# A hybrid decoder layer on one Trainium2 core: a second copy of x with columns as rows, and 1 / rms sent through DRAM

## The reference, cut to what matters

```python
h = rmsnorm(x, ln_gain)                      # x: 2048 tokens x 1024 channels
z = einsum('bsd,de->bse', h, w_in)           # 1024 -> 4608 columns
q, k, v, g_attn, x_lru, g_lru = split(z)
y_attn = rmsnorm(swa_sink_attention(rope(q), rope(k), v, sinks) * silu(g_attn), attn_out_gain)
u      = causal_depthwise_conv(x_lru, conv_w, conv_b)
y_lru  = rmsnorm(rg_lru(u, gates) * silu(g_lru), lru_out_gain)
x      = x + concat([y_attn, y_lru]) @ w_out
out    = rmsnorm(x, final_gain)
# rmsnorm(x, g) = x * rsqrt(mean(x * x) + EPS) * g, per token
```

## Time and profile before

| | |
|---|---|
| median of 3 runs | 1374.45 us |
| profiled execution | 1375.38 us |
| its span, first to last instruction | 1373.7 us |
| PE busy | 1353.7 us (99%) |
| DVE busy | 970.2 us (71%) |
| ACT busy | 845.6 us (62%) |
| granted TensorE clock | 0.998 of full speed |

### The profile page before, as it was taken

The page is one execution under the profiler, slowest core; times in us unless marked ns, Lnnn a source line. Parts: engine busy times, 40 slices in busy tenths (PEclk is TensorE's granted clock), DMA queues, the critical chain, the costliest instruction groups (busy, mean ns, idle before and its releaser), DMA issues.

```text
span 1373.7 us, 22283 instructions
## 1 busy us (share of the span) xinstructions
PE 1353.7 (99%) x6756; PEld 1107.4 (81%) x6756; DVE 970.2 (71%) x1668; ACT 845.6 (62%) x1729; POOL 217.2 (16%) x247
## 2 busy tenths in 40 slices
PE   8999999999999999999999999999989999999998
PEld 7777877888888888888888878888867888888886
DVE  5998999968686877868687767878686544434442
ACT  7888797867777685867777585766764221222120
POOL 2020212112130312113031212213020000000000
PEclk9999999999999999999999999999999999999999
DMA  8766768655554555454555655354535423324120
GB/s 323 260 226 246 274 225 288 230 188 173 183 178 177 203 184 200 158 187 172 184 186 184 224 202 211 135 206 164 193 114 193 138 86 97 98 86 121 62 92 31
DMA packets 98289, 243.22 MB, mean 177 GB/s; under 512 B 8112, under 2 KB 43056, under 8 KB 98224
## 3 DMA queue, kind: packets, MB, share of 16 engines
q1 hardware_dynamic: 91200, 217.79, 46.9%
q0 software_dynamic: 7024, 24.65, 4.5%
HBM read 179.49 MB, written 62.91 MB: 176 GB/s over the span
## 4 chain that ended last, share of the span: by engine, by line
PE 85%; DVE 3%; ACT 2%; issue 1%; DMA 1%; DVEq 0%; ACTq 0%; POOL 0%; POOLq 0%
PE ring L1548 50%; PE acc_b L223 12%; PE ring L223 11%; PE ps_tv L1611 4%; PE ps_s L1587 3%; PE ps_tv L1598 2%; PE ring L1625 2%; PE ps_tv L1587 1%; PE ring L1635 1%; DMA y_scratch<-ya 1%; PE ring L1560 0%; DMA w_raw<-w_out_d 0%; DVE o_sb L1318 0%; PE acc_b L1998 0%; DVE cu L1340 0%
## 5 line engine op out<-in xcount | busy, mean ns | idle before, releaser
L1548 PE MATMUL ring<-split,w_hi 128*128 128x512 f32 x2288 | 717.1, 395 | 1.1 <-DVE w_lo L1082 0.4
L1548 PEld LDWEIGHTS ring<-split,w_hi 128*128 128x128 f32 x2288 | 421.3, 188 | 97.5 <-issue 8.9
L1548 PE MATMUL ring<-split,w_lo 128*128 128x512 f32 x1144 | 446.6, 390 | 0.0
L1548 PEld LDWEIGHTS ring<-split,w_lo 128*128 128x128 f32 x1144 | 214.7, 188 | 45.9
L663 POOL TENSOR_SCALAR_AFFINE_SELECT p_hi_c<-p_hi 128x512 fp32r<-128x512 f32 x64 | 41.5, 648 | 518.1 <-ACT p_hi L891 518.1
L883 ACT ACTIVATE p_sb<-s_sb,smax 128x129 f32<-128x129 f32 x256 | 99.6, 392 | 0.6
L1840 ACT ACTIVATE w_hi<-res 128x1024 fp32r<-128x1024 f32 x15 | 15.9, 1060 | 132.3 <-DVE res L1913 132.3
L223 PE MATMUL acc_b<-wo_rest,y_own 128*128 128x512 f32 x384 | 90.8, 393 | 5.4 <-DVE rms L1898 4.3
L223 PE MATMUL ring<-split,y_own 128*128 128x512 f32 x384 | 91.5, 392 | 0.0
L1340 DVE SCALAR_TENSOR_TENSOR cu<-xl,prm,cu 128x512 f32<-128x512 f32 x96 | 72.2, 752 | 26.6 <-ACT cu L910 20.0
L223 PEld LDWEIGHTS acc_b<-wo_rest,y_own 128*128 128x128 f32 x384 | 72.2, 189 | 21.3 <-DVE rms L1898 4.4
(11 more groups left out here) (249 smaller groups left out, 2420.5 us busy)
## 6 DMA issues: line engine op xcount, KB each, us to landing
w_hi<-w_split_scratch SPq DMA_DIRECT2D x108, 512.0 KB, 3.3
w_lo<-w_split_scratch SPq DMA_DIRECT2D x108, 512.0 KB, 4.3
w_raw<-w_tiles_d SPq DMA_DIRECT2D x36, 512.0 KB, 4.3
w_split_scratch<-w_hi SPq DMA_DIRECT2D x36, 512.0 KB, 5.0
w_split_scratch<-w_lo SPq DMA_DIRECT2D x36, 512.0 KB, 5.7
y_scratch<-hs POOLq DMA_DIRECT2D x32, 256.0 KB, 6.2
y_scratch<-ya POOLq DMA_DIRECT2D x16, 512.0 KB, 6.0
rows<-y_scratch SPq DMA_DIRECT2D x8, 1024.0 KB, 7.8
```

Source lines behind the costliest of these rows:

```text
L1548: last = mm(bank(r), w[:, i % WSLOTS, k, :], h[:, par, k, :], start=(k == 0 and j == 0), stop=(k == KC - 1 and j == 2))
```

## The change

The input is given a second time, as `x_turned`, laid out on the host with the 128 channels of a piece on the partitions and the tokens along the rows. SP now loads a block of both forms (two transfers of 512 KB instead of one). The first form only serves the sum of squares. The second one, `xt`, takes the half of `rows` in which the gain lay, and is normalised where it is: 1 / rms, one number for each of 128 tokens on the partitions, must become a row on every partition. It is stored to DRAM and read back to all partitions (`rs_row`), and DVE multiplies in eight instructions of 128x128, one for each piece, with the gain as a scalar per partition. ACT and DVE then split `xt` in SBUF. The turns on TensorE in the bodies, their two places in the ring and the load of the gain go away.

```diff
-    xb = both.rows[:, 0, :];  gain_row = both.rows[:, 1, :]
+    xb = both.rows[:, 0, :];  xt = both.rows[:, 1, :].rearrange("p (k t) -> p k t", k=KC)
             def load_x(g, q):
                 sp.dma_start(xb, x[0, bass.ds((g + (q + 1) * KV) * P, P), :]).then_inc(*x_in.one())
+                sp.dma_start(xt, x_turned[bass.ds(g + (q + 1) * KV, 1), :, :, :].rearrange("o p k t -> p (o k) t")
+                             ).then_inc(*x_in.one())
                 load(GA0)
+                if q < NQUART - 1:
+                    sp.wait_ge(*x_rs.at(n, 1))
+                    sp.wait_ge(*x_norm.at(n, 0))
+                    sp.dma_start(rs_dram.rearrange("o p -> p o"), xs[:, 3:4]).then_inc(*rs_kept.one())
                 load(GA1)
+                if q < NQUART - 1:
+                    sp.wait_ge(*rs_kept.at(n, 1))
+                    sp.dma_start(rs_row[:, :], rs_dram.broadcast_to([P, P])).then_inc(*rs_in.one())
                 load(GL1)
...
                 if x_follows(q, nxt_par != par):
-                    sp.wait_ge(*ring_ready.at(n, R_XT1 + 1))
+                    sp.wait_ge(*h_low.at(n, 2))
                     load_x(following, q + (nxt_par != par))
...
             def square_x(n):
-                act.wait_ge(*x_in.at(n, 1))
+                act.wait_ge(*x_in.at(n, 2))
...
+            def invert_x(n):
+                dve.wait_ge(*x_root.at(n, 0))
+                dve.wait_ge(*rs_kept.at(n, 0))
+                nc.vector.reciprocal(xs[:, 3:4], xs[:, 2:3]).then_inc(*x_rs.one())
             def norm_x(n):
-                dve.wait_ge(*x_root.at(n, 0))
-                nc.vector.reciprocal(xs[:, 3:4], xs[:, 2:3]).then_inc(*x_rs.one())
-                dve.wait_ge(*x_rs.at(n, 1))
-                stt(out=xb, in0=xb, scalar=xs[:, 3:4], in1=gain_row, op0=ALU.mult,
-                    op1=ALU.mult).then_inc(*x_norm.one())
+                dve.wait_ge(*x_in.at(n, 0))
+                dve.wait_ge(*rs_in.at(n, 1))
+                for c in range(KC):
+                    last = stt(out=xt[:, c, :], in0=xt[:, c, :], scalar=prm[:, C_GAIN, c:c + 1], in1=rs_row[:, :],
+                               op0=ALU.mult, op1=ALU.mult)
+                last.then_inc(*x_norm.one())
...
                 sink_in()
+                if q < NQUART - 1:
+                    invert_x(n)
                 conv(0)
...
                 lru_tail(0)
-                lru_scan(0)
                 if split_next:
                     split_w(n, KVG)
+                lru_scan(0)
...
                 turn_p(0)
-                if q < NQUART - 1:
-                    turn_x()
                 score(3)
...
                 if nxt_par != par:
-                    pe.wait_ge(*ring_dve.at(n, FREED_BY_DVE.index(R_XT1) + 1))
+                    pe.wait_ge(*h_low.at(n, 2))
```

More of the change, by code:

```diff
@@ L112, in two @@
         return self.sem, 2 * self.unit
-    def three(self):
-        self.count += 3
-        return self.sem, 3 * self.unit
     def checked(self, bodies, beyond=0):
@@ L280, in phase_a @@
     xb = both.rows[:, 0, :]
-    gain_row = both.rows[:, 1, :]
+    xt = both.rows[:, 1, :].rearrange("p (k t) -> p k t", k=KC)
     h_hi = both.split[:, :, 0, :].rearrange("p q (k t) -> p q k t", k=KC)
@@ L391, in phase_a @@
         ring_dve = signal("ring_dve", len(FREED_BY_DVE))
-        x_in = signal("x_in", 1, 16, ahead=1)
+        x_in = signal("x_in", 2, 16, ahead=2)
+        rs_kept = signal("rs_kept", 1, 16)
+        rs_in = signal("rs_in", 1, 16)
         x_sq = signal("x_sq", 1, ahead=1)
@@ L457, in phase_a @@
         yl_out = [signal(f"yl_out{u}", 1) for u in range(UNITS)]
-        bank = lambda r: ring[:, r % RING, :]
+        bank = lambda r: ring[:, BANK[r], :]
         f = lambda ap: ap.bitcast(F32)
@@ L473, in bank_free @@
         def bank_free(n, r):
-            before = (r - RING) % NR
-            late = 0 if r >= RING else 1
+            before = IN_FRONT[r] % NR
+            late = 0 if IN_FRONT[r] >= 0 else 1
             if before in FREED_BY_ACT:
@@ L753, in exp_table, with high_x @@
                 nc.scalar.activation(table_sink[:, :], ones[:, :], ACT.Exp).then_inc(x_early_root, 1)
-            def high_x(dst, col, half, ps, ready, done):
-                act.wait_ge(*ready)
+            def high_x(n, dst, col, half):
+                part = slice(half * 4, half * 4 + 4)
+                act.wait_ge(*x_norm.at(n, 1))
                 act.sem_inc(settled, 1)
-                nc.scalar.activation(dst[:, half * 4:half * 4 + 4, bass.ds(col, P)],
-                                     ps.rearrange("p (k t) -> p k t", k=4), ACT.Copy).then_inc(*done)
+                nc.scalar.activation(dst[:, part, bass.ds(col, P)], xt[:, part, :], ACT.Copy).then_inc(*h_high.one())
             act.wait_ge(zeroed, 1)
@@ L1352, in silu_l @@
                               op0=ALU.add, op1=ALU.mult)
-                    if u and q == NQUART - 1:
-                        ins.then_inc(*ring_dve.three())
-                    else:
-                        ins.then_inc(*ring_dve.one())
+                    ins.then_inc(*ring_dve.one())
                 def one_less(u):
@@ L1539, in project_first, with project @@
                 last.then_inc(*ring_ready.one())
-            def project(n, i, par, split, turned=True):
+            def project(n, i, par, split):
                 r = RING_OF_GROUP[i]
@@ L1549, in project @@
                                   start=(k == 0 and j == 0), stop=(k == KC - 1 and j == 2))
-                if turned:
-                    last.then_inc(*ring_ready.one())
-                else:
-                    last.then_inc(*ring_ready.three())
+                last.then_inc(*ring_ready.one())
             def turn_v(n):
@@ L1627, in gates @@
                                 ins.then_inc(*ring_ready.one())
-                def turn_x():
-                    pe.wait_ge(*x_norm.at(n, 1))
-                    for half in range(2):
-                        pe.wait_ge(*bank_free(n, R_XT0 + half))
-                        for k in range(4):
-                            c = half * 4 + k
-                            last = nc.tensor.transpose(bank(R_XT0 + half)[:, k * P:(k + 1) * P],
-                                                       xb[:, c * P:(c + 1) * P], ident[:, :])
-                        last.then_inc(*ring_ready.one())
                 project(n, XL0, par, split)
@@ L2106, in laid_out @@
             gates[:, half, :, :, (j + half) % 2, :] = blocks[:, :, half].transpose(0, 2, 1, 3)
-    return {"channel_params": np.stack([by_unit(v) for v in rows], axis=1),
+    x_turned = np.asarray(inputs["x"])[0].reshape(NTOK, P, KC, P).transpose(0, 3, 2, 1)
+    return {"x_turned": x_turned, "channel_params": np.stack([by_unit(v) for v in rows], axis=1),
             "out_gains": np.concatenate([by_unit(inputs["attn_out_gain"]), by_unit(inputs["lru_out_gain"])], axis=1),
```

49 lines of the change are left out of this document (24 added, 25 removed).

## The result

The changed kernel takes 1423.1 us (median of 4 runs, 1422.71 to 1425.05), the kernel before beside it 1374.47 us: 1.0358 times as long, 95% interval 1.0343 to 1.0372. The forecast had 1375.9 us and a range up to 1382.0. It is off by 47 us.

The account below looks back on a forecast made before the run. TensorE bounds bodies 4 to 11, a ring of ACT and DVE quarter 0. Gain 6.4 us from the turns, losses 5.7 (bodies 0 to 2) and 2.1 (body 3): +1.4, 1375.9 us; range 1368.5 to 1382.0.

Parts of the forecast that it names:

- the new wait on SP: Quarter 0: GA1's load and XL1's stores stand behind the reciprocal's wait; 1.4 us added in bodies 0 to 2, 2.4 late in body 3.
- it lands 5.6 us later, at +7.7: Body 1: XL1's second store lands 5.6 us after issue, +7.7 from L1270's start; only then may ACT split GA1.
- the sum: Whole kernel: -6.4 + 5.7 + 2.1 = +1.4 us, so 1374.45 becomes 1375.9; near-cancellation had chance 0.55.
- rival (c): SP's queue: the small store's 128 pieces delay the burst behind it; with 1.5 us, +7.4, 1381.9 us; chance 0.2.
- none of the three can make it up: Quarter 0: ACT, DVE and TensorE can't recover the added 1.4 us before DVE reaches the next body.
- That the splits read SBUF and not PSUM I take as nothing: Splits of x on ACT and DVE: same count, DVE's pair still 1.28 us, so no cost.
- The turns: TensorE, bodies 4 to 11: 7.0 us saved, less 0.3 at each of two quarter ends, gain 6.4; quarter 0 nothing.
- The multiplications: DVE's normalisation as eight instructions: 1.6 to 2.3 us for one of 1284 ns, 0.4 more taken, hidden behind ACT's root.
- The scan's place: DVE, bodies 0 to 2: swapping scan and KVG's split costs 0.5 us each, bounds 0 to 0.7.
- The row in quarters 1 and 2: The row's trip through DRAM has some 7 us to spare there, so costs nothing.
- The late load of x: Bodies 0 to 2: next XL0 load some 3 us later, hidden by ACT's wait for Q0; without that wait, part would show.
- The bounds: Near-cancellation: landing 5.2 to 6.2 us, swap 0 to 0.7, multiplications up to 0.3 a body; -2.5 to +6, 1372 to 1380.5 us.

Follow-up runs that it names:

- runs 3: Changed kernel without the row's store, read-back and SP's waits for them; the multiplications read ones: 1380.46 us.
- 14: Changed kernel with the row stored as one 512-byte piece, and both its store and read-back moved behind the load of GL1: 1381.31 us.
- 13: Changed kernel with the row stored as one 512-byte piece, and only its read-back, with the wait for the landing, behind the load of GL1: 1394.16 us.
- run 1: Changed kernel with the row (of ones) stored as one piece of 512 bytes, not 128 pieces of 4 bytes: 1396.81 us.
- run 2: Kernel before plus a store, behind GA0's load, of 128 pieces of 4 bytes into a DRAM row nobody reads: 1382.22 us.
- Run 10: Kernel before with the late load of x, and DVE's two subtractions for x's remainder reading their first operand from SBUF, not PSUM: 1379.91 us.
- run 4: Kernel before without the eight turns of x on TensorE in a body, all else kept: 1369.73 us.
- run 12: Changed kernel with the row made on TensorE behind XL1, scan ahead of KVG's split again, and x split earlier on ACT and DVE: 1369.49 us.
- run 6: Kernel before with DVE's one multiplication of x done as eight of 128x128: 1374.39 us.
- run 7: Kernel before with DVE's split of KVG ahead of the first scan instead of behind it: 1376.72 us.
- run 5: Kernel before with SP's next load of x waiting for DVE's remainder of the present block, not for TensorE's turn: 1374.33 us.
- 15: Kernel of run 12 with KVG's split placed directly ahead of x's split on both ACT and DVE: 1366.89 us.

## Why the prediction was wrong, step by step

**Where the 48.6 us are.** By the chain of runs 3, 14, 13, 1 and the changed kernel: 6.1 us without the trip, 0.9 for its transfers, 12.9 for the wait for the reciprocal, 2.6 for the wait for the landing, 26.3 for the pieces. The order in which they are taken away matters: the pieces by themselves cost 7.8 us (run 2).

**The step that failed** is the third bullet of the new wait on SP, "it lands 5.6 us later, at +7.7", with what the sum makes of the time. Two things were wrong in it.

- The landing: 12.4 us and not 5.6, by the pieces in one row of DRAM. This is rival (c), which had the right mechanism (the small store ahead of the burst in the queue) and a price of 1.5 us a body, a choice between nothing and the 1.1 and 5.7 us of a burst of 512 KB transfers. The runs have 26.3 / 4 = 6.6 us a body, above all of these. The bounds of the unknown operation were taken from transfers that have nothing of its kind; it had no upper bound in the trace.
- The clock: the sum took a wait of TensorE at its own length. With a normal landing the wait itself was as forecast (ACT 2.96 us for 2.8, TensorE 2.74 for 2.2), but the time was not: 1.4 us in bodies 0 to 2 and 2.4 in body 3 make 6.6 us, and runs 13 and 14 have 12.9. By the bodies of run 1 against run 14 it is 1.8, 5.7, 1.5 and 5.3 us. The idle time that was added, 6.2 us, is near the forecast's 6.6; the 8.1 us of busy time at a lower clock were no term of it. In body 1 TensorE is busy 5.3 us longer at a clock of 0.91, and in body 3 it waits 3.98 us and is busy 1.7 us longer. In the changed kernel TensorE is busy 260.8 us in quarter 0 against 247.4 in run 14, with the same work at clock 1.00: 13 of the 52 us.

The step behind these, "none of the three can make it up", held.

**"That the splits read SBUF and not PSUM I take as nothing"** failed too. The row that stood behind it, 0.69 us for an SBUF instruction at 197.47, was of a moment when GpSimd doesn't multiply. Run 10 prices it at 5.3 us; in the changed kernel bodies 4 to 11 gain 3.3 us where run 4 has 5.5 and run 12, with the pair clear of GpSimd, 6.3; it also holds a part of the 9.7 us by which quarter 0 is longer without the trip.

**The turns**: -5.5 us in bodies 4 to 11 for -6.4 (run 4; -4.7 by the medians); at the ends of quarters all of it is lost and not 0.3 us. Right in kind.

**The multiplications**: 2.18 us for the eight, inside the forecast's 1.6 to 2.3 though above the 1.6 to 1.7 that it took, and hidden (run 6): right. **The scan's place**: 2.1 to 2.2 us for 1.5 (run 7): right in kind, and at the upper end of the 0 to 0.7 us a body that it allowed. **The row in quarters 1 and 2**: the stalls are there too, with 4 KB packets of 4.5 to 6.7 us, and those bodies are shorter all the same: right.

**The late load of x**: nothing by itself (run 5), but the forecast's condition, "without that wait to hide in", came true. With the pair slower by 1.5 us, SP issues XL0's load later still, and ACT waits 3.8 to 4.4 us near the end of bodies 0 to 2 of runs 3 and 14 for the stores issued with it. What part of quarter 0's 9.7 us is this was not tried by itself: order and pair account for 2.2 + 3.8, and 3.7 us stay open. Runs 12 and 15 narrow it down: they keep the second load of x and the eight multiplications, have x split early and none of these waits of ACT, and their quarter 0 is 254.6 and 252.0 us. So load and multiplications cost little by themselves; what costs is tied to the late place of the pair.

**The bounds** don't add up as written: landing, swap and multiplications at their ends give -2.1 to +7.6 us, and it has -2.5 to +6. Its landing of 5.6 us is 5.7 in the row it names. Neither matters beside 47 us.

## What to carry to other kernels

A column to a row through DRAM is not a small transfer: 128 pieces of 4 bytes into one row of 512 bytes held up what stood behind them in the queue, and some of what stood ahead. As one piece, or 512 bytes apart, they did not. One turn on TensorE of the column read 128 times does the same in 0.3 us, if it is put where the column is already there. When an operand moves from PSUM to SBUF, look at what GpSimd does at that moment. And a wait of TensorE can cost more than its length, because its clock may fall behind it; a bound for an operation that the trace doesn't show must not come from rows of another kind.

## What the runs showed that was not expected

- 128 writes of 4 bytes into one 512-byte row of DRAM: at most 9 ns each in their own records, and behind them 4 KB packets, of the queue of SP and of that of GpSimd, that take up to 7.1 us (8.0 in run 2). The same writes 512 bytes apart: 2.0 us at most, and no time to be measured.
- DVE's two subtractions of 128x512: 1.28 us with one operand in PSUM, 2.4 to 2.8 with both in SBUF beside GpSimd's multiplication, 1.28 again with both in SBUF at a moment without that multiplication. Neither engine's row shows an idle time for it; only the durations differ.
- In run 1 a wait of 2.7 us on TensorE and one of 1.5 us later in the same body were each followed by 6.8 us at half the full clock; the body had 0.91 in place of 1.00 and 5.3 us more of busy time. A wait of 2.5 us in another body of the same run was followed by no fall at all.
